# A feed-forward's tiles placed inside the expert turns that come before it

## What is computed

```python
def hierarchical_moe(h, w_group, b_group, w_expert, b_expert, w_gate, w_up, w_down):
    ...
    for e in range(N_EXPERTS):
        hid = jax.nn.silu(t @ w_gate[e]) * (t @ w_up[e])
        y = y + combine[:, e:e + 1] * (hid @ w_down[e])

def swiglu(x, w_gate, w_up, w_down):
    return (jax.nn.silu(x @ w_gate) * (x @ w_up)) @ w_down

def macaron_ffn(xs, g, shift, scale, gate, w_gate, w_up, w_down):
    return xs + 0.5 * gate * swiglu(modulate(xs, g, shift, scale), w_gate, w_up, w_down)

# second_block, layer 0
x_lat = macaron_ffn(x_lat, norm_g[i, 0], m[0], m[1], m[2], ffn_w_gate[i, 0], ffn_w_up[i, 0], ffn_w_down[i, 0])
x_ctx = macaron_ffn(x_ctx, norm_g[i, 0], mc[0], mc[1], mc[2], ffn_w_gate[i, 0], ffn_w_up[i, 0], ffn_w_down[i, 0])
```

## Time and profile before

| | us |
|---|---|
| median of 3 runs | 2291.49 (2289.32 to 2292.2) |
| the profiled execution | 2287.71 |
| its span, first to last instruction | 2285.8 |
| TensorE busy in the span | 2107.9 |

### The profile page before, as it was taken

One profiled execution on the slowest core, in us unless ns is written; L12 is line 12 of the kernel. 1 busy time (PEld: TensorE's weight loads), 2 busy tenths in 40 slices (PEclk: granted clock), 3 DMA queues, 4 the chain that ended last, 5 costly groups with the idle time before them and its releaser, 6 DMA issues. The chain is left out here.

```text
span 2285.8 us, 30473 instructions
## 1 busy us (share of the span) xinstructions
PE 2107.9 (92%) x12174; PEld 1593.3 (70%) x12174; DVE 1223.8 (54%) x2031; ACT 836.1 (37%) x1412; POOL 21.9 (1%) x36
## 2 busy tenths in 40 slices
PE   7999999889997666799999999999999999999998
PEld 6787678654442222388888888757888888888887
DVE  1276235451110000277777774466777777877776
ACT  1102144311000000265465453246555544545444
POOL 1000000000000000000000001000000000000000
PEclk9999999989998787799999999999999999999999
DMA  9988784369999999955554455104465554454351
GB/s 364 400 333 341 304 298 181 147 239 421 420 421 421 421 421 421 383 190 208 174 178 163 159 189 160 33 1 161 134 221 166 184 178 153 168 196 165 114 189 37
DMA packets 219349, 540.59 MB, mean 236 GB/s; under 512 B 8895, under 2 KB 122137, under 8 KB 194633
## 3 DMA queue, kind: packets, MB, share of 16 engines
q1 hardware_dynamic: 216456, 531.69, 62.3%
q0 software_dynamic: 2192, 6.57, 1.1%
q10 hardware_dynamic: 560, 0.38, 0.1%
HBM read 537.56 MB, written 1.05 MB: 236 GB/s over the span
## 5 line engine op out<-in xcount | busy, mean ns | idle before, releaser
L1075 PE MATMUL lo<-xs,wp 128*128 128x512 f32 x3904 | 694.8, 340 | 14.9 <-DVE wp L2236 8.4
L1075 PEld LDWEIGHTS lo<-xs,wp 128*128 128x128 f32 x3904 | 599.6, 189 | 109.2 <-issue 16.3
L826 ACT ACTIVATE wp<-ring 128x1024 fp32r<-128x1024 f32 (+1 forms) x500 | 404.1, 832 | 309.8 <-PE hi L1075 180.5
L2236 DVE TENSOR_TENSOR wp<-ring,wp 128x1024 fp32r<-128x1024 f32 (+1 forms) x500 | 459.7, 939 | 3.0 <-ACT wp L826 2.9
L1075 PE MATMUL lo<-ring,scratch 128*64 128x512 f32 (+1 forms) x1536 | 301.5, 724 | 93.6 <-DMA ring<-in_moe_w_up_dram 35.2
L1075 PE MATMUL hi<-hs,wp 128*128 128x512 f32 x2016 | 370.8, 342 | 3.6 <-DVE hs L2485 3.2
L1075 PEld LDWEIGHTS hi<-hs,wp 128*128 128x128 f32 x2016 | 311.3, 189 | 50.7 <-DVE hs L2485 3.5
L1075 PEld LDWEIGHTS lo<-ring,scratch 128*64 128x64 f32 (+1 forms) x1536 | 89.2, 143 | 297.0 <-issue 281.1
L1075 PE MATMUL lo<-ht,ring 128*128 128x256 f32 (+1 forms) x640 | 134.9, 370 | 5.6 <-DVE ring L2441 1.6
L1075 PEld LDWEIGHTS lo<-ht,ring 128*128 128x128 f32 x640 | 116.9, 190 | 26.8 <-ACT ht L990 4.8
L2196 DVE TENSOR_TENSOR scratch<-scratch,lo 128x512 f32<-128x512 f32 x12 | 13.0, 1081 | 227.6 <-PE lo L1075 227.6
(11 more groups left out here) (425 smaller groups left out, 2153.1 us busy)
## 6 DMA issues: line engine op xcount, KB each, us to landing
ring<-in_mod_w_dram SPq DMA_DIRECT2D x72, 1024.0 KB, 13.8
ring<-in_moe_w_gate_dram SPq DMA_DIRECT2D x64, 1024.0 KB, 18.6
ring<-in_moe_w_up_dram SPq DMA_DIRECT2D x64, 1024.0 KB, 19.1
ring<-in_moe_w_down_dram SPq DMA_DIRECT2D x64, 1024.0 KB, 17.9
ring<-in_ffn_w_gate_dram SPq DMA_DIRECT2D x55, 1024.0 KB, 5.9
ring<-in_ffn_w_up_dram SPq DMA_DIRECT2D x55, 1024.0 KB, 9.1
ring<-in_ffn_w_down_dram SPq DMA_DIRECT2D x50, 1024.0 KB, 10.0
ring<-in_w_in_dram SPq DMA_DIRECT2D x20, 1024.0 KB, 14.1
```

The costliest lines, as they stand in the source:

```text
L826: act.activation(wp[:, q % SLOTS, 0, k:k + w.shape[1], :], w, ACT.Copy).then_inc(piece_hi, 2 // len(parts))
L1075: return pe.matmul(dst, lhsT, rhs, start=start, stop=stop, **kw)
L2236: tt(wp[:, q % SLOTS, 1, k:k + w.shape[1], :], w, wp[:, q % SLOTS, 0, k:k + w.shape[1], :].bitcast(F32), ALU.subtract).then_inc(piece_lo, ...
```

## The change

- 18 of the 22 tiles and the first two down passes of the context's feed-forward are made inside the four quad turns: 12 pieces in each (`early_piece`), and 4 more after the last turn. `early(q)` says what piece q is: of each 24, 16 are those of eight tiles and 8 a down pass.
- A quad turn has 15 ring units instead of 12. An even turn (the first and third) takes three units of tiles, at places 0, 5 and 10; an odd one takes a unit of tiles at place 0 and two down units at 5 and 6.
- An early piece has its rounded weights in one of two places (`home_0`, `home_1`), and its rest is written over the weights in the ring. A step is three matmuls of 256 columns into one half of a bank, `hi[:, 2]` or `hi[:, 3]`, so that no halves are added. The remaining pieces use `wp` with the same three matmuls (`late_step`).
- Since the sum over turns no longer has its banks, each quad turn's sum is scattered in two halves (`scatter_rows`, into `hi[:, 0:2]`) and added to `x` by VectorE (`x_summed`).
- The context's input is rounded in the third turn of pairs. The norm of `x`, before made beside tiles 0 to 16, stands beside tiles 18 to 21 and the last down pass.
- Some scratch places move, and GpSimd loads `window` and `lam_in` after the turns.

```diff
 U_FFN = [0] * 5
-U_FFN[0] = U_MOE + 3 * EXPERTS
-U_FFN[1] = U_FFN[0] + FFN_UNITS
+EARLY_TILES = 18
+EARLY_PIECES = 52
+U_QUADS = U_MOE + 6 * PAIRS
+U_FFN[0] = U_QUADS + 15 * QUADS
+U_FFN[1] = U_FFN[0] + 5
...
-            return U_MOE + 6 * PAIRS + 12 * (i - PAIRS) + 4 * j + 2 * half + pair
+            return U_QUADS + 15 * (i - PAIRS) + ((1, 3, 6, 8, 11, 13), (1, 3, 7, 9, 11, 13))[i % 2][2 * j + half] + pair
...
+            if f == 0:
+                return U_FFN[0] + c - 8 if c > 7 else U_QUADS + 15 * (c // 4 * 2 + c % 4 // 3) + (0, 5, 10, 0)[c % 4]
...
+        def early(q):
+
+            u, r = q // 24, q % 24
+            if r < 16:
+                return u, 8 * u + r // 2, r % 2, None
+            return u, None, None, r - 16
...
+        def early_bank(q):
+
+            _, tile, a, d = early(q)
+            return hi[:, 2 + (a if d is None else d % 2), 0:T]
...
+            def early_units(i, block):
+
+                u, second = (i - PAIRS) // 2, i % 2
+                if not second and block % 2 == 0:
+                    gate_up(up_unit(0, 8 * u + block), (0, 0), 4 * u + block // 2)
+                if second and block == 0:
+                    gate_up(up_unit(0, 8 * u + 6), (0, 0), 4 * u + 3)
+                if second and block == 2:
+                    for j in range(2):
+                        down(down_units(0, u)[j], (0, 0), 4 * u + 2 * j, 2)
...
+            def early_round(q):
+
+                if q >= 2:
+                    act.wait_ge(piece_done, q - 1)
+                parts = early_weights(q)
+                for n, w, home, _, _ in parts:
+                    wait_unit(act, n)
+                    act.activation(home, w, ACT.Copy).then_inc(piece_hi, 2 // len(parts))
...
+            for i in range(PAIRS, EX_TURNS):
+                q = 12 * (i - PAIRS)
+                for j in range(4):
+                    early_piece(q + j, j < 2)
+                early_round(q + 4)
+                early_round(q + 5)
+                expert_silu(i)
+                for j in range(4, 11):
+                    early_piece(q + j, j < 10)
+                expert_turned(i)
+                early_piece(q + 11, False)
+                early_round(q + 12)
+                early_round(q + 13)
+                expert_out(i)
+            for q in range(EARLY_PIECES - 4, EARLY_PIECES):
...
+            def early_piece(q):
+
+                u, tile, a, d = early(q)
+                if q == 0:
+                    pe.wait_ge(x_ready, 2 * TT + 1)
+                    pe.wait_ge(xn_lo, KC)
+                pe.wait_ge(piece_lo, 2 * q + 2)
+                if d is None:
+                    if tile:
+                        pe.wait_ge(h_mul, tile)
+                    if u and tile == 8 * u:
+                        pe.wait_ge(ev_done, KC * u)
+                else:
+                    pe.wait_ge(h_lo, 8 * u + 8)
+                    if d >= 2:
+                        pe.wait_ge(ev_done, KC * u + d - 1)
+                parts = early_weights(q)
+                for n, _, home, rest, at in parts:
+                    frees = d == KC - 1 or (tile is not None and tile % 2 == 1 and a == 1)
+                    many = home.shape[1]
+                    for k in range(many):
+                        ends = at + k == KC - 1
+                        rhs, c = (xs if d is None else hs), at + k
+                        dst = early_bank(q)
+                        if k == many - 1:
+                            ins = mm(dst, rest[:, k, :], rhs[:, c, 0], False, False, skip_group_check=True)
+                            if frees:
+                                ins.then_inc(unit_used[n % RING], 1)
+                        mm(dst, home[:, k, :], rhs[:, c, 0], c == 0, False, skip_group_check=True)
+                        ins = mm(dst, home[:, k, :], rhs[:, c, 1], False, ends, skip_group_check=True)
+                        if ends:
+                            ins.then_inc(piece_done, 1)
+                        elif k < many - 1:
+                            mm(dst, rest[:, k, :], rhs[:, c, 0], False, False, skip_group_check=True)
...
+            def scatter_rows(i, t):
+
+                if i == EX_TURNS - 1 and t == 0:
+                    pe.wait_ge(ex_yd, 2 * EX_TURNS)
+                    pe.wait_ge(ex_ylo, 2 * EX_TURNS)
+                    pe.wait_ge(ex_back, EX_TURNS)
+                pe.wait_ge(x_ready, x_sums(i, t) - 1)
+                for h in range(2):
+                    for a in range(2):
+                        ins = mm(hi[:, h, :], back_r[:, t * P:t * P + P], y_split[:, a, h * 512:h * 512 + 512], a == 0, a == 1, skip_group_check=True)
+                ins.then_inc(ex_done, 1)
...
+            for i in range(PAIRS, EX_TURNS):
+                q = 12 * (i - PAIRS)
+                second = i % 2
+                for j in range(4):
+                    early_piece(q + j)
+                if i > PAIRS:
+                    pe.wait_ge(ex_yd, 2 * i)
+                    pe.wait_ge(ex_ylo, 2 * i)
+                    pe.wait_ge(ex_back, i)
+                    scatter_rows(i - 1, 0)
+                pe.wait_ge(ex_hg, 2 * i + 2)
+                expert_up(i, 0, 0)
+                expert_up(i, 0, 1)
+                if i > PAIRS:
+                    scatter_rows(i - 1, 1)
+                for j in range(4, 12 if second else 8):
+                    early_piece(q + j)
+                pe.wait_ge(ex_back, i)
+                expert_up(i, 1, 0)
+                expert_up(i, 1, 1)
+                if not second:
+                    early_piece(q + 8)
+                    early_piece(q + 9)
                 if i + 1 < EX_TURNS:
                     pe.wait_ge(ex_onehot, i + 2)
                     gather()
-                pe.wait_ge(ex_hd, i + 1)
-                for f in range(4):
-                    ins = pe.transpose(lo[:, 0, f * P:f * P + P], ex_h[:, f * P:f * P + P], ident)
-                ins.then_inc(ex_turned, 1)
-                pe.wait_ge(ex_weighted, i + 1)
+                if not second:
+                    early_piece(q + 10)
...
+            early_piece(EARLY_PIECES - 4)
+            scatter_rows(EX_TURNS - 1, 0)
+            early_piece(EARLY_PIECES - 3)
+            scatter_rows(EX_TURNS - 1, 1)
+            early_piece(EARLY_PIECES - 2)
+            early_piece(EARLY_PIECES - 1)
+            pe.wait_ge(rt_flag, 2)
+            with pe.If(pe.value_load(overflow[0:1, 0:1], min_val=0, max_val=1)):
...
+            for tile in range(EARLY_TILES, FTILES):
+                pe.wait_ge(h_mul, tile - 1)
+                for a in range(2):
+                    q = up_q(0, tile, a)
+                    pe.wait_ge(piece_lo, 2 * q + 2)
+                    for k in range(KC):
...
+            def x_summed(i, t):
+
+                dve.wait_ge(ex_done, 1 + TT * (i - PAIRS) + t + 1)
+                tt(x[:, t, :], x[:, t, :], hi[:, 0:2, :].rearrange("p a n -> p (a n)"), ALU.add).then_inc(x_ready, 1)
+
+            def early_rest(q):
+
+                dve.wait_ge(piece_hi, 2 * q + 2)
+                parts = early_weights(q)
+                for n, w, home, rest, _ in parts:
+                    tt(rest, w, home.bitcast(F32), ALU.subtract).then_inc(piece_lo, 2 // len(parts))
...
+            early_rest(0)
+            early_rest(1)
+            dve.wait_ge(ex_done, 1)
+            tt(x2, x2, hi[:, :, :], ALU.add).then_inc(x_ready, 1)
+            for i in range(PAIRS, EX_TURNS):
+                q = 12 * (i - PAIRS)
+                expert_places(i)
+                for j in range(4):
+                    early_piece(q + j, j < 2)
+                if i > PAIRS:
+                    x_summed(i - 1, 0)
+                early_rest(q + 4)
+                early_rest(q + 5)
+                if i > PAIRS:
+                    x_summed(i - 1, 1)
+                for j in range(4, 8):
+                    early_piece(q + j, True)
+                if i % 2:
+                    for j in range(8, 12):
+                        early_piece(q + j, j < 10)
+                    expert_hidden(i)
+                    expert_back(i)
+                else:
+                    expert_hidden(i)
+                    for j in range(8, 11):
+                        early_piece(q + j, j < 10)
+                    expert_back(i)
+                    early_piece(q + 11, False)
+                early_rest(q + 12)
+                early_rest(q + 13)
+                expert_rest(i)
+            early_piece(EARLY_PIECES - 4, True)
+            x_summed(EX_TURNS - 1, 0)
+            early_piece(EARLY_PIECES - 3, True)
+            dve.wait_ge(ex_done, 1 + TT * QUADS)
+            tt(x[:, 1, :], x[:, 1, :], hi[:, 0:2, :].rearrange("p a n -> p (a n)"), ALU.add).then_inc(moe_done, 1)
...
```

359 lines of the change are left out of this document (234 added, 125 removed).

## The result

| | before | after |
|---|---|---|
| median, us | 2290.4 (4 runs, 2281.8 to 2292.2) | 2247.3 (4 runs, 2242.8 to 2254.7) |
| ratio | 1 | 0.9832 (95%: 0.9810 to 0.9854) |
| profiled execution, us | 2287.71 | 2248.36 |
| its span | 2285.8 | 2246.6 |

The account below looks back on a forecast made before the run. Transfers were taken to bound the quad turns, TensorE the context's first feed-forward. +68.7 + 16.2 + 84 - 216.5 = -47.6 us took 2287.71 to 2240.1; 3.8 for the median gave 2244 us, range 2211 to 2272.

Parts of the forecast that it names:

- What bounds each stage: Quad turns bound by transfers with 85 us of free TensorE; the context's first feed-forward bound by TensorE with free transfers.
- the added transfers (+68.7): Quad turns: 8 gate and up units at 6.01 us and 4 down units at 5.14 add 68.7 us.
- The ring (+16.2): Odd quad turns: down units held through eight pieces stop the DMA engines 8.1 us in each of two turns, 16.2 us.
- slack of 9 us: Quad turns: TensorE's 66.3 us of work leaves it 9 us a turn against the transfers' 75 to 78.
- TensorE's term: Quad turns: 0.122 us per matmul, 2.93 a piece, 66.3 us a turn, so TensorE fits beside the transfers.
- rivals of the clock (2264): Quad turns: mean clock stays 0.77, four turns take 344.4 us, total 2264 us; chance 0.19, including something in between.
- of the loads (2314): Rival in early pieces: weight loads don't overlap, 0.234 us per matmul, a piece 5.6, total 2314 us; chance 0.04.
- The rival of unbroken transfers: Quad turns: transfers never stop, only the 68.7 us of added transfers stand, total 2228 us; chance 0.17.
- The end: From the last expert weight to the second feed-forward: 84 us instead of 216.5, bounds 76 and 95.
- VectorE has per column ... 2.75 us: Last down pass: VectorE needs 2.75 us per column against TensorE's 2.5, 22 us in all.
- What costs nothing: Moved input rounding, per-turn sums into x and GpSimd's two later loads are covered; some 5 us if the covers failed.
- The sum: Whole kernel: +68.7 + 16.2 + 84 - 216.5 = -47.6 us, giving a median of 2244 us.

Follow-up runs that it names:

- e5: Changed kernel with the quad turns' eight gate and up units loaded from 4 KB rows instead of 1 KB (wrong weights); 2248.2 us, ratio 0.9816.
- e1: Changed kernel with each odd-turn down unit holding 512 columns of all eight hidden tiles, so the first frees after four pieces, not eight; 2237.7 us, ratio 0.9787.
- e2: Changed kernel with one product per step repeated in the 16 down pieces of the odd quad turns, 128 extra matmuls; 2267.9 us, ratio 0.9905.
- e3: Changed kernel with 128 extra matmuls in the first eight tile pieces of each even quad turn; 2255.2 us, ratio 0.9862.
- e8: Changed kernel with two weight loads per early step instead of three, same 768 columns, half of the 512 left out of the sum; 2247.2 us, ratio 0.9808.
- e4: Changed kernel with 18 idle matmuls before the down pieces of the two odd quad turns; 2247.2 us, ratio 0.9825.
- e6: e1 kernel with 10 idle matmuls before the down pieces of the two odd quad turns; 2235.8 us, ratio 0.9759.
- e7: e1 kernel with idle matmuls between the last two expert blocks, before the first remaining early piece and after the branch; 2237.6 us, ratio 0.9773.

## Why the prediction was right

- **What bounds each stage, and the added transfers (+68.7).** Right. The turns last as long as their transfers, and the surcharge of short rows is there: -5.7 of -7.0 us in e5.
- **The ring (+16.2).** Right. Two holes of 8.9 and 8.8 us, in the second and the fourth turn and in no other; e1 takes nearly all of them away and gains 15.3 us, e2 adds 15.6 us of work in them and loses 15.7.
- **The turns came out 4.4 us longer (+89.3 for +84.9).** Both down units land and are rounded 7.4 us after TensorE has run out of work, not 5, and the holes are 1.5 us longer together. A pair of turns, from one request after a hole (851.96) to the next (1015.55), is 163.6 where 77.8 + 84.2 = 162.0 were foreseen: 3.2 for two pairs. The rest, about 1, fits GpSimd's two loads (1.3). That even turns stay full held in the changed kernel, but their slack of 9 us is not to be had everywhere: e3 adds 3.9 us ahead of one request of the first turn and loses 3.2.
- **TensorE's term.** Right in size: a down piece 2.88 for 2.93, the wait between tiles 0.61 for 0.6, a mean clock of 0.91 for over 0.9. Its reason was wrong: "there the loads set the pace" does not carry over, since e8 has a third of the loads less and a piece is only 0.05 us shorter. The 0.122 came out because the columns take 0.120; that is luck. The rivals of the clock (2264) and of the loads (2314) are out by these numbers and e8. (What spoke for the clock's rival was read too strongly: the page's first slice has TensorE at 7 tenths and the clock at 9.) The rival of unbroken transfers is out by the two holes. Without them it would have been near: in e1 the two middle parts are 54 us shorter than before, where it had 63.8.
- **The end (84, measured 85.6).** Right in the sum, by two errors that cancel. Ready at 8.43 for 8.5; early pieces done at 22.4 for 25.2, since the clock was up again when they began (1.00 from 1049 to 1055 us); the late ones start at 27.2 for 28.5, with a branch of 4.8 for 3.3; the last down pass starts at 57.1 for 60.9 and takes 28.6 for 23. The step that failed here is "VectorE has per column ... 2.75 us": it adds up one engine's work and overlooks the ring through ScalarE.
- **What costs nothing.** No cost of the moved rounding is to be seen. Two covers failed in part. The first sum into `x` does not sit beside matmuls: TensorE waits 2.60 us for it. And GpSimd's loads do not find a DMA share of about a half: they are requested before the turns end, at a share of 1.0, and some 1.3 us of transfers are missing where they land. The kernel before requested them at 499.9 and 500.5 us, so what the move costs on balance is open; none of these was taken out by itself.
- **The sum.** -40.3 in the two parts (89.3 - 129.6) for -47.6, and 43 in the medians. 4.4 come from the turns, 1.7 from the end, 1.3 from the old feed-forward, which the first trace had 2.5 us longer than the second. That the median came within 4 us of the 2244 is in part luck: the parts outside the change differ by more than that between two executions.

## What to carry to other kernels

Work moved under transfers brings transfers and holds buffers: ask of each unit in a ring how long it is held and which request stands behind it, and cut the data so that a unit is free after half of its uses. TensorE's time counted one to one where the down units were held (15.7 us for 15.6) and a fifth of that elsewhere (3.2), so the same microsecond has two prices in one stage; even there it was a request behind a used unit that made it count. Where two engines hand work to each other in every step, add up the ring through both and not each by itself; putting one operation a step later can open it.

## What the runs showed of the hardware

- A third weight load and a cut of 512 columns into two of 256 cost 0.05 us in a piece of 8 steps (2.88 in the changed kernel, 2.83 in e8): these loads over the full height are hidden behind the columns.
- Units with rows of 1, 2, 4 and 8 KB arrived at 349, 387 (e1), 408 and 421 GB/s (the kernel before, 714 to 914 us).
- Parts with the same instructions differ by up to 11 us between two executions of one kernel, ahead of the turns. Part of it goes with the clock: from the request of `conv_w_out` to that of `xa_w_o` the first trace of before takes 123.6 us at a granted clock of 1.00 (202 to 326 us), the second 129.5 at 0.95 (205 to 335 us). What decides it is open.
- Two loads of 128 KB, asked for while the queue was full, came with a dip from 422 to 195 GB/s over 2 us (1032 to 1034) as they landed.
- Fillers paid where something waited for the engine: 4.4 us with the full hold (e4), 1.0 in e6, none before a wait for a unit that lands late anyway (e7).
